# Prompt attention of a hybrid decoder step: probabilities turned in the two row halves of the array, value products after every job, query tiles in the order 1, 3, 0, 2

## The reference, cut to what matters

```python
def masked_softmax(s, valid):
    s = jnp.where(valid, s, NEG)
    m = jnp.max(s, axis=-1, keepdims=True)
    p = jnp.where(valid, jnp.exp(s - m), 0.0)
    den = jnp.sum(p, axis=-1, keepdims=True)
    return p / jnp.maximum(den, 1e-30), m, den

s = jnp.einsum('bnqgrd,bnkgd->bgrnqk', qb, kg) * SCALE
s = s - slopes_gr[:, :, None, None, None] * dist.astype(jnp.float32)
p, _, _ = masked_softmax(s, valid)
return jnp.einsum('bgrnqk,bnkgd->bnqgrd', p, vg).reshape(B, S, G, R, Dh)
```

## Time and profile before

| | |
|---|---|
| median of 3 runs | 2277.27 us |
| lowest, highest run | 2275.46, 2282.76 us |
| profiled execution, span | 2281.8 us |
| run nearest to that span | 2282.76 us (0.96 us more than the span) |
| mean granted TensorE clock | 0.964 of 2.4 GHz |
| PE busy | 2099.0 us (92%), 14522 instructions |
| PEld busy | 1538.6 us (67%) |
| DVE, ACT, POOL busy | 1093.1, 731.9, 440.5 us |
| prompt attention | from 430.4 to 676.8 us of the span |

### The profile page before, as it was taken

How to read it: one execution, slowest core, us unless ns; L and a number is a source line. 1 busy time by engine, 2 the same in 40 slices (tenths; PEclk the granted TensorE clock), 3 DMA queues, 4 the chain that set the end, 5 groups by cost and what they waited for, 6 DMA issues and landing times. The chain is left out here.

```text
span 2281.8 us, 37014 instructions
## 1 busy us (share of the span) xinstructions
PE 2099.0 (92%) x14522; PEld 1538.6 (67%) x14522; DVE 1093.1 (48%) x2549; ACT 731.9 (32%) x1517; POOL 440.5 (19%) x454
## 2 busy tenths in 40 slices
PE   8999999888989587899888999889999999999898
PEld 7888888644447465788656654468778887878543
DVE  3111211356655233333666533266777777687322
ACT  0000011366653222122344420034545445454300
POOL 5422333234440001343333310000000000000000
PEclk9999999999999788999999999989999999999999
DMA  6333123221149997644344456149998999999630
GB/s 163 125 100 94 59 79 79 58 71 42 43 173 418 415 381 265 247 187 184 130 171 170 171 151 155 48 136 318 286 310 267 313 294 311 302 285 318 232 147 23
DMA packets 214571, 440.67 MB, mean 193 GB/s; under 512 B 60640, under 2 KB 173808, under 8 KB 197760
## 3 DMA queue, kind: packets, MB, share of 16 engines
q1 hardware_dynamic: 206944, 362.46, 48.6%
q0 software_dynamic: 7456, 75.86, 9.2%
HBM read 411.58 MB, written 165.23 MB: 253 GB/s over the span
## 5 line engine op out<-in xcount | busy, mean ns | idle before, releaser
L2144 PE MATMUL three<-x1T,arena 128*128 128x256 f32 x768 | 206.8, 397 | 3.7 <-DVE rec_qq L2534 3.7
L2442 POOL TENSOR_TENSOR rec_v_own<-rec_rows,row_own 64x512 f32<-64x512 f32 x16 | 16.6, 1038 | 727.8 <-PE rec_bX L2259 594.5
L580 POOL TENSOR_TENSOR pab_w<-pab_w 128x512 f32<-128x512 f32 (+2 forms) x76 | 112.1, 1475 | 220.1 <-PE pab_bZ L368 129.3
L2144 PEld LDWEIGHTS three<-x1T,arena 128*128 128x128 f32 x768 | 137.3, 193 | 19.0 <-DVE rec_qq L2534 4.1
L1479 PE MATMUL cmp_bH<-cmp_xT,cmp_w 128*128 128x256 f32 x512 | 132.3, 384 | 0.5 <-DVE qd L1553 0.5
L817 ACT ACTIVATE ap_sc<-ap_sc,ap_nmax 128x128 f32<-128x128 f32 (+1 forms) x192 | 106.2, 554 | 82.6 <-DVE ap_nmax L847 81.4
L847 DVE CUSTOM_DVE_ANT_0 ap_sc<-ap_bS,ap_bias 128x128 f32<-128x128 f32 (+1 forms) x192 | 86.5, 488 | 67.8 <-PE ap_bS L762 32.2
L1520 DVE COPY cmp_xT<-cmp_bT 128x512 f32<-128x512 f32 x80 | 55.3, 692 | 108.5 <-PE cmp_bT L1468 108.3
L785 PEld LDWEIGHTS ap_bT<-ident,ap_sc 128*128 128x128 f32 x480 | 52.5, 142 | 76.0 <-POOL ap_sc L881 67.8
L785 PE MATMUL ap_bT<-ident,ap_sc 128*128 128x128 f32 x480 | 73.4, 284 | 30.5 <-ACT ap_pT L832 19.1
L1479 PEld LDWEIGHTS cmp_bH<-cmp_xT,cmp_w 128*128 128x128 f32 x512 | 89.0, 193 | 8.1 <-issue 0.9
(11 more groups left out here) (486 smaller groups left out, 4675.3 us busy)
## 6 DMA issues: line engine op xcount, KB each, us to landing
out<-in_cache_a_k SPq DMA_DIRECT2D x8, 8160.0 KB, 29.7
out<-in_cache_a_v SPq DMA_DIRECT2D x8, 8160.0 KB, 29.5
arena<-in_w_in_c SPq DMA_DIRECT2D x64, 512.0 KB, 6.6
sa_ring<-in_cache_a_v SPq DMA_DIRECT2D x25, 1024.0 KB, 11.7
arena<-in_cache_a_k SPq DMA_DIRECT2D x23, 1024.0 KB, 13.7
sa_ring<-in_cache_a_k SPq DMA_DIRECT2D x17, 1024.0 KB, 23.8
arena<-in_cache_a_v SPq DMA_DIRECT2D x15, 1024.0 KB, 24.2
pab_w<-in_w_in_ab SPq DMA_DIRECT2D x128, 64.0 KB, 2.3
```

The costliest lines, as they stand in the source:

```text
L580: nc.gpsimd.tensor_tensor(to, a, b, op).then_inc(sums, 1)
L2144: last = nc.tensor.matmul(bank[:, 0:SEQ // 2], left[:, k, :], right[:, k, :], start=(first and k == 0), stop=(k == 3), skip_group_check=True)
```

## The change

Five things are changed, all in `attend_prompt`:

1. **Turns in row halves.** The two heads' 128 x 128 transposes become 64 x 128 pieces: rows 0 to 63 of a piece of `sc` go through the upper row half of the array into bank `bT[0]`, rows 64 to 127 through the lower half into `bT[1]`. So there are twice as many transposes (960 for 480), each with 64 moving columns for 128. A turn waits for both heads' scaling and for both banks at once, and signals at its end.
2. **Copies** take one bank each, thus one half of the queries of both heads (as many elements as before), and ScalarE's stands ahead of its exponentials in the step.
3. **Value products job by job**, at step i + BEHIND (5): for each key tile and head one product of 128 query columns. Per unit 20 products of 128 columns take the place of 8 of 512 to 128; the columns are 2560 both ways.
4. **Query tiles in the order 1, 3, 0, 2** (sizes 2, 4, 1, 3).
5. **Scores a job ahead**: in step i TensorE does the turn of job i - 3, the scores of job i + 1, then the keys, then the value products of job i - 5.

`pT` becomes four buffers of one job each; `pv_done` counts jobs.

```diff
-    LAG, RING = 3, 4
+    LAG, RING, TURNED, BEHIND = 3, 4, 4, 5
+    ORDER = (1, 3, 0, 2)
...
-        pT = [[s.sb(f"pT{u}{h}", [P, TILES, SEQ]) for h in range(2)] for u in range(2)]
+        pT = [s.sb(f"pT{u}", [P, 2 * SEQ]) for u in range(TURNED)]
...
-            u, m = divmod(i, TILES)
+            u, m = i // TILES, ORDER[i % TILES]
...
+        def half_of(i, half):
+            return pT[i % TURNED][:, 0:2 * job(i)[2]].rearrange("p (b q) -> p b q", q=P)[:, :, HD * half:HD * half + HD]
+        STEPS = range(-4, NJ + BEHIND + 1)
...
+                def turn(i):
+
+                    u, m, cols = job(i)
+                    pe.wait_ge(p_ready, 2 * i + 2)
+                    if place[i]:
+                        pe.wait_ge(t_read[0], place[i])
+                    if i:
+                        pe.wait_ge(t_read[1], i)
+                    for h in range(2):
+                        for j in range(m + 1):
+                            for half in range(2):
+                                r, at = slice(HD * half, HD * half + HD), (h * (m + 1) + j) * HD
+                                last = nc.tensor.transpose(bT[half][:, at:at + HD], sc[i % RING][h][r, j * P:(j + 1) * P], ident[r, r])
+                                if h == 1 and j == m:
+                                    last.then_inc(t_done[half], 1)
+
+                def turn_keys(u):
...
+                def weigh(i):
+                    u, m, cols = job(i)
+                    kind, p, grp = UNITS[u]
+                    pe.wait_ge(t_read[0], place[i] + 1)
+                    pe.wait_ge(t_read[1], i + 1)
+                    out = bO[grp % 2]
+                    if i % TILES == 0:
                         if kind != "W" and grp >= 2:
                             pe.wait_ge(o_read, grp - 1)
                         if kind == "S":
                             for h in range(2):
                                 nc.tensor.matmul(out[HD * h:HD * h + HD, :], vd[:, h, p, :], pTc[h][:, :], start=True, stop=False)
-                        for j in range(TILES):
-                            for h in range(2):
-                                if kind == "A":
-                                    own = kv[1][:, j, p * P + HD * h:p * P + HD * h + HD]
-                                else:
-                                    c = {"S": VS - KC, "W": VW - KC}[kind] + HD * h
-                                    own = kv_b[:, j, c:c + HD]
-                                last = nc.tensor.matmul(out[HD * h:HD * h + HD, j * P:], own, pT[u % 2][h][:, j, j * P:],
-                                                        start=(kind == "A" and j == 0), stop=(kind != "S" and j == TILES - 1))
-                        last.then_inc(pv_done, 1)
+                    for j in range(m + 1):
+                        for h in range(2):
+                            if kind == "A":
+                                own = kv[1][:, j, p * P + HD * h:p * P + HD * h + HD]
+                            else:
+                                c = {"S": VS - KC, "W": VW - KC}[kind] + HD * h
+                                own = kv_b[:, j, c:c + HD]
+                            last = nc.tensor.matmul(out[HD * h:HD * h + HD, m * P:(m + 1) * P], own, pT[i % TURNED][:, h * cols + j * P:h * cols + (j + 1) * P],
+                                                    start=(kind == "A" and j == 0), stop=(j == m and (kind == "A" or kind == "W" and i % TILES == TILES - 1)))
+                    last.then_inc(pv_done, 1)
+
+                for i in STEPS:
+                    if 0 <= i - LAG < NJ:
+                        turn(i - LAG)
+                    if 0 <= i + 1 < NJ:
+                        scores(i + 1)
+                    ku = keys_step(i)
+                    if ku is not None:
+                        turn_keys(ku)
+                    if 0 <= i - BEHIND < NJ:
+                        weigh(i - BEHIND)
 
             @block.scalar
             def _(act):
                 for i in STEPS:
+                    if 0 <= i - LAG < NJ:
+                        j = i - LAG
+                        u, m, cols = job(j)
+                        act.wait_ge(t_done[0], place[j] + 1)
+                        if j >= TURNED:
+                            act.wait_ge(pv_done, j - TURNED + 1)
+                        nc.scalar.copy(half_of(j, 0), bT[0][:, 0:cols].rearrange("p (b q) -> p b q", q=HD)).then_inc(t_read[0], 1)
                     if 0 <= i < NJ:
                         u, m, cols = job(i)
                         for h in range(2):
@@ -824,13 +849,6 @@
                         nc.scalar.copy(keys_of(ku)[:, :], bT[0][:, :]).then_inc(t_read[0], 1)
                         act.wait_ge(t_read[0], keys_place[ku] + 1)
                         act.sem_inc(key_ready, 1)
-                    if 0 <= i - LAG < NJ:
-                        u, m, cols = job(i - LAG)
-                        act.wait_ge(t_done[0], place[i - LAG] + 1)
-                        if u >= 2:
-                            act.wait_ge(pv_done, u - 1)
-                        nc.scalar.copy(pT[u % 2][0][:, 0:m + 1, m * P:(m + 1) * P],
-                                       bT[0][:, 0:cols].rearrange("p (j q) -> p j q", q=P)).then_inc(t_read[0], 1)
 
             @block.vector
             def _(dve):
@@ -838,12 +856,13 @@
                     if 0 <= i < NJ:
                         u, m, cols = job(i)
                         kind, p, grp = UNITS[u]
-                        if m == 0 and kind != "W":
+                        if i % TILES == 0 and kind != "W":
                             dve.wait_ge(bias_in[grp % 2], 16 * (grp // 2) + 16)
                         for h in range(2):
                             dve.wait_ge(s_done, 2 * i + h + 1)
-                            if i >= RING:
-                                dve.wait_ge(t_done[h], (place[i - RING] if h == 0 else i - RING) + 1)
+                            if i >= RING and h == 0:
+                                dve.wait_ge(t_done[0], place[i - RING] + 1)
+                                dve.wait_ge(t_done[1], i - RING + 1)
                             nc.vector.tensor_tensor_reduce(out=sc[i % RING][h][:, 0:cols], in0=bS[i % 2][h][:, 0:cols],
                                                            in1=bias[grp % 2][:, h, SEQ - cols:SEQ], scale=-1.0, scalar=3e38,
                                                            op0=ALU.add, op1=ALU.min,
@@ -854,18 +873,19 @@
                             dve.wait_ge(p_ready, 2 * (i - 1 - RING) + 2)
                         nc.vector.reciprocal(rden[:, (i - 1) % RING, :], den[:, (i - 1) % RING, :]).then_inc(den_ready, 1)
                     if 0 <= i - LAG < NJ:
-                        u, m, cols = job(i - LAG)
-                        dve.wait_ge(t_done[1], i - LAG + 1)
-                        if u >= 2:
-                            dve.wait_ge(pv_done, u - 1)
-                        nc.vector.tensor_copy(pT[u % 2][1][:, 0:m + 1, m * P:(m + 1) * P],
-                                              bT[1][:, 0:cols].rearrange("p (j q) -> p j q", q=P)).then_inc(t_read[1], 1)
-                    u = done_unit(i - 1)
-                    if u is not None and UNITS[u][0] != "S":
+                        j = i - LAG
+                        u, m, cols = job(j)
+                        dve.wait_ge(t_done[1], j + 1)
+                        if j >= TURNED:
+                            dve.wait_ge(pv_done, j - TURNED + 1)
+                        nc.vector.tensor_copy(half_of(j, 1), bT[1][:, 0:cols].rearrange("p (b q) -> p b q", q=HD)).then_inc(t_read[1], 1)
+                    if 0 <= i - BEHIND - 1 < NJ and (i - BEHIND - 1) % TILES == TILES - 1:
+                        u = (i - BEHIND - 1) // TILES
                         kind, p, grp = UNITS[u]
-                        dve.wait_ge(pv_done, u + 1)
-                        g = gT[0 if kind == "A" else 1][:, p, :]
-                        nc.vector.tensor_tensor(g, bO[grp % 2][:, :], g, ALU.mult).then_inc(o_read, 1)
+                        if kind != "S":
+                            dve.wait_ge(pv_done, TILES * u + TILES)
+                            g = gT[0 if kind == "A" else 1][:, p, :]
+                            nc.vector.tensor_tensor(g, bO[grp % 2][:, :], g, ALU.mult).then_inc(o_read, 1)
                 dve.wait_ge(o_read, 16)
 
             @block.gpsimd
```

More of the change, by code:

```diff
@@ L721, in keys_step @@
             return i // TILES + 1 if i % TILES == 0 and i // TILES + 1 in KEYS_OF else None
-        def done_unit(i):
-            return (i - LAG - 1) // TILES if 0 <= i - LAG - 1 < NJ and (i - LAG - 1) % TILES == TILES - 1 else None
-        STEPS = range(-4, NJ + LAG + 2)
+        def half_of(i, half):
+            return pT[i % TURNED][:, 0:2 * job(i)[2]].rearrange("p (b q) -> p b q", q=P)[:, :, HD * half:HD * half + HD]
+        STEPS = range(-4, NJ + BEHIND + 1)
         with nc.Block() as block:
@@ L744, in _ @@
                         store(grp - 4)
```

(25 more changed lines are left out.)

56 lines of the change are left out of this document (9 added, 47 removed).

## The result

| | before | changed |
|---|---|---|
| median | 2278.28 us (2275.46 to 2282.76, 4 runs) | 2226.47 us (2223.79 to 2231.07, 4 runs) |
| ratio | | 0.977, 95% interval 0.9751 to 0.9789 |
| profiled execution, span | 2281.8 us | 2223.8 us |
| mean granted clock | 0.964 | 0.965 |

The change takes 51.8 us off the median, for 55 forecast; 2226.47 lies in the range, 4.5 us over the point.

The account below looks back on a forecast made before the run. The stage was taken as bound by TensorE's order: its work plus a loop scores, bias, exponentials, copy, turn. 61.6 + 120.8 + 9 = 191.4 us for 246.4, 55 us less: 2222 us, range 2212 to 2256.

Parts of the forecast that it names:

- What bounds it: Changed stage: bound by TensorE's order, 16.9 us work in a 19.03 us pair plus a loop through scores and copies.
- A pair of half transposes at 0.065 us: Turns: both row halves run side by side, so a unit's 20 pairs take 1.30 us for 2.14.
- Rival 1: Turns: a pair of half transposes costs 0.11 to 0.13 us, giving 2243 to 2253 us; chance 0.19.
- Borders: Time between TensorE's blocks beyond their columns: 0.10 turn, 0.10 scores, 0.15 products, 1.40 us a unit.
- The waits: TensorE's waits in the stage: nearly gone, 0.15 us a unit added, giving 15.1 us a pair, 7.7 an A unit.
- rival 2: Chains across engines bind: half of today's waits stay, 2243 us, or 2259 with today's borders; chance 0.16.
- the comparison of 3.0 to 3.2 us with 3.4: Tightest chain, from size-1 turn to next turn but one: 3.0 to 3.2 us, against 3.4 for TensorE's two steps.
- Start and end of the stage: Time outside the stage's steady units: 7.5 us before, 9 us after the change.
- only the last job's products stand alone: Stage end: products lie two jobs further behind, but one job's stand alone, not the 2.37 us of a unit.
- rival 3: Next stage: its DMA runs late anyway, so little gain is carried on, 2270 to 2277 us; chance 0.03.
- rival 4: Changed stage: the clock falls to 1.2 GHz under row-half transposes, 2302 us at three fifths of it; chance 0.04.

Follow-up runs that it names:

- full_turns: The changed kernel with whole 128 x 128 transposes again, one bank per head, all else as changed: 2257.22 us, ratio to before 0.9916.
- halves_alone: The kernel before with only the turns in row halves and which half each copy takes changed: 2266.05 us, ratio 0.9949.
- copy_behind: The changed kernel with ScalarE's copy moved behind the exponentials of its step, as before: 2239.06 us, ratio 0.9827.
- by_two: The changed kernel with the value products of two jobs together in every second step, six buffers for turned pieces: 2232.87 us, ratio 0.98.
- scores_first: The changed kernel with the scores of job i ahead of the turn, instead of those of job i + 1 behind it: 2254.53 us, ratio 0.99.
- halves_apart: The changed kernel with each turn doing all pieces of the upper row half first, then those of the lower: 2238.72 us, ratio 0.9827.

## Why the prediction was right, point by point

**What bounds it.** Right. Starts added up gave 16.9 us of work in a pair of 19.03, and the change had to beat both the work and the loop. full_turns and halves_alone show what each part gives alone: 21 us for the order, 13 for the turns.

**A pair of half transposes at 0.065 us.** Right, and the step on which 0.89 of the 1.54 us a unit of full_turns rest. 1.44 us of turns in a unit are 20 pairs at 0.0625 = 1.25 and four borders of 0.05. In the records the two transposes of a pair start 1 to 7 ns apart and pairs 62 ns apart, with loads of 128 columns. Rival 1 falls. By the load rule of the Trainium skill ("TensorE: Matmul & The Clock Gate", section "LDWEIGHTS (loading the stationary operand)") a pair would have been 0.107; the measurement decides against it for these transposes.

**Borders.** The sum was right, its parts less so: turns 0.05 for 0.10 forecast, scores (2.76 - 2.13) / 4 = 0.16 for 0.10, products 0.165 for 0.15 (2.79 us in the S unit from 567.75 on, which has no compressed product, less 2.13, over four). Together 0.37 a job for 0.35. A unit is 1.44 + 2.76 + 2.79 = 6.99 us for 6.96 forecast, the pair 14.84 for 14.8 of work. The records show where the borders lie. The first score product starts 56 to 60 ns behind the last pair of a turn, no more than from pair to pair: both are in row halves, and between them there is no border. The 0.05 of a turn is its first step, 112 ns for 62; scores and products have such a first step too. Where the form changes, the last products of 128 columns stand 0.20 us ahead of the next block for 0.11 from one to the next, so 0.10 more. Against full_turns a turn's border fell by 0.11 (0.16 there) and that of scores by 0.05 (0.21 there, all of the difference in their first step); products pay 0.165 in both. "TensorEngine Tiling (Array Packing)" of the Trainium skill, section "Key Properties", says that changing the tiling mode drains the engine; the trace agrees as far as it can show it, with 0.10 us at the end of a block where the form changes and nothing where it doesn't.

**The waits.** This term was mis-sized: I added 0.15 us a unit, and 0.15 for ScalarE in A units; the windows show none. 7.57 us for 7.7, 14.84 for 15.1: 8 x (0.13 + 0.26) = 3.1 us too much. But rival 2 was near: copy_behind, by_two and scores_first each lengthen a chain by one block and at once show waits at turns (0.57, 0.15 to 0.23 and 0.62 us in the units looked at). The chain is just under TensorE's sum, as the comparison of 3.0 to 3.2 us with 3.4 had it.

**Start and end of the stage.** 9 us forecast. First scores to last gating is 431.23 to 618.49 = 187.3 us, less 8 x (7.57 + 14.84) = 179.3: 8.0 us. What failed here is the step "only the last job's products stand alone". First, behind the last turn TensorE has the products of three jobs in one row, 1.97 us for 2.37 of a whole unit's before. Second, TensorE does not set the end. The timelines of TensorE, GpSimd and SyncE, in the changed kernel:

```profile
615.79 1.97 PE L812 MATMUL ap_bO<-ap_pT,kv_b 128*64 128x128 f32 x32
...
615.01 4.44 POOL L620 DMA_DIRECT2D out<-scratch_z  x8
...
618.52 0.32 SPq L734 DMA_DIRECT2D scratch_h<-gT  x1
```

and in the kernel before:

```profile
670.14 4.44 POOL L620 DMA_DIRECT2D out<-scratch_z  x8
...
679.32 0.33 SPq L1180 DMA_DIRECT2D sa_bias<-in_bias_a_s  x1
```

GpSimd issues eight copies of outputs behind its last scaling and waits for them. The next stage started 9.2 us behind that before (679.32) and starts 8.6 us behind it now (623.64). Gating ends 5.15 us ahead of the next stage's first load for 2.56 before, so 2.6 us of the earlier end are lost. The stage from first scores to last gating became 59.1 us shorter (246.4 to 187.3); it began 0.8 us later; 59.1 - 0.8 - 2.6 is the 55.7 us at L1200. So that the forecast of 55 came out to 0.7 us is luck: the stage itself became 4.1 us shorter than forecast (the waits that were not there, and 1.0 at start and end), and 0.8 + 2.6 us were lost outside of it.

What the copies cost was not tried by itself, but all fourteen profiled kernels speak for them. From GpSimd's first copy to the next stage's first load it is 7.7 to 9.2 us in every one. From the end of gating it is 1.1 us (halves_alone) to 5.2, so in most of them gating had long been done.

**Rivals 3 and 4.** Everything behind moved by 55.7 us or slightly more, so rival 3 falls. The clock is 1.00 in the steady part with twice as many transposes as before, so rival 4 falls. That alone does not test what a clock makes of transposes, since products fill 5.5 of a unit's 7.0 us. The start of the next stage, in the changed kernel, does; windows (columns as in the earlier trace rows) and timeline of PE:

```profile
623.64:629.90 6.26, 6.22 (x36) 5.90 (x36) 3.84 (x6) 1.76 (x3) 0.00 (x0) 0.50 0.82 273
629.95:631.70 1.75, 1.56 (x13) 1.29 (x12) 1.54 (x3) 0.90 (x2) 0.00 (x0) 1.00 0.94 351
```

```profile
623.67 1.94 PE L1296 MATMUL sa_bT<-ident,arena 64*128 64x64 f32 x16 [5.92 <-PEq L729]
625.54 4.53 PE L1242 MATMUL sa_bT<-ident,arena 128*128 128x128 f32 x20
```

The clock goes from 0.50 (1.2 GHz) to 1.00 (2.4 GHz) at 629.9 us, when TensorE had done nothing but transposes since its idling of 5.92 us. "TensorE: Matmul & The Clock Gate" of the Trainium skill, Part 4 ("PE-mode transpose"), says that transposes don't count as activity and don't bring the full clock; these rows differ for fp32 transposes. They show a price of the longer idling too: the same sixteen transposes took 1.19 us before, behind 3.33 us of it, and take 1.94 now. The next stage did not become longer by it.

**The median.** The stage gave 55.7 us; the medians differ by 51.8 in one comparison and 55.9 in the other. The kernel's own spread (2220.75 to 2231.07 over nine runs) covers that.

## What to carry to other kernels

Add up starts, not busy times, and set them beside the longest loop across engines: here work (16.9 of 19.03 us a pair) and loop were both near the bound, so shorter turns alone gave 13 us, a better order alone 21, and both 52. Put blocks of the same array form next to each other, and spread products with no hurry between the blocks that others wait for, rather than in one piece. Before counting on an earlier end, look at what each engine does behind its last work in the stage: here 2.6 us were lost there, most likely to eight copies on GpSimd's queue.

## What the runs showed of the hardware that was not expected

- Transposes in the two row halves start out of the program's order. In halves_apart the lower half's first starts 0.30 us behind the upper's, with three of the upper's eight still to start, and a score product passes three transposes. "TensorE: Matmul & The Clock Gate" of the Trainium skill, Part 3 ("Packing small matmuls — row/col tiling"), has products strictly in program order in start and end; these rows differ for products in different row groups. In this kernel each half signals with a semaphore of its own.
- An fp32 transpose of 64 x 128 with 64 moving columns takes 62 ns from start to start (in halves_apart the upper half alone steps so), and the same with the other row half beside it: 128 x 128 in 0.0625 us by two halves, for 0.107 to 0.109 by one full transpose (full_turns).
- Between a turn and scores, both in row halves, there is no border: 56 to 60 ns from the last pair to the first score product, where pairs are 62 ns apart. A change of form costs 0.10 us behind the last product, and a block's first step another 0.05.
- The granted clock rose from 0.50 to 1.00 over fp32 transposes alone (623.67 to 629.9 us).
